# Delta-rule stage: joined scratch rows, a shared ring of gate weights, and another order of filler and block inversions

## The reference, cut to what matters

```
h = x + norm(W_o[ sig(gates_a) * (attention . W_a) + sig(gates_b) * (deltanet . W_b) ])
y = h + norm(relu(norm(h) W_1)^2 W_2)
```

```
lower = where(strict, beta * (k k^T) * decay, 0)
tinv  = (lower + I)^-1
u, w  = tinv @ (v * beta),  tinv @ (k * beta * exp(gc))
step:   v_new = u - w @ state
        o     = q_dec @ state + (q k^T * decay) @ v_new
        state = state * exp(g_last) + k_dec^T @ v_new
```

## Time and profile before

| what | value |
|---|---|
| median of 3 runs | 2793.87 us (2791.05 to 2799.13) |
| profiled execution, its own time | 2795.2 us |
| span from first to last instruction | 2793.4 us |
| mean granted clock of PE | 0.955 |
| PE busy over the span | 2533.9 us, 91% |
| DVE, ACT, POOL busy over the span | 1306.7, 863.4, 567.5 us |
| DMA, mean over the span | 134 GB/s |

### The profile page before, as it was taken

How to read it: one execution, slowest core, us unless ns; L and a number is a source line. 1 busy time by engine, 2 the same in 40 slices (tenths; PEclk the granted TensorE clock), 3 DMA queues, 4 the chain that set the end, 5 groups by cost and what they waited for, 6 DMA issues and landing times. The chain is left out here.

```text
span 2793.4 us, 33654 instructions
## 1 busy us (share of the span) xinstructions
PE 2533.9 (91%) x12600; PEld 2113.3 (76%) x12600; DVE 1306.7 (47%) x1688; ACT 863.4 (31%) x1415; POOL 567.5 (20%) x499
## 2 busy tenths in 40 slices
PE   6999999797989997998498894799999979999998
PEld 5888888686879895776287683688888768887887
DVE  5665125265635336887633433744444342234332
ACT  4333323251111115776300332322222142133221
POOL 2352236341212110000520231221121000000000
PEclk9999999898999999999599897999999989999999
DMA  4232212585555643221644554232232273345443
GB/s 142 72 91 87 77 53 106 166 260 185 163 158 170 177 135 144 102 102 68 226 141 147 198 176 168 73 98 79 89 97 79 76 254 103 115 145 206 162 150 106
DMA packets 308213, 373.38 MB, mean 134 GB/s; under 512 B 53240, under 2 KB 234616, under 8 KB 303480
## 3 DMA queue, kind: packets, MB, share of 16 engines
q1 hardware_dynamic: 216152, 293.97, 32.8%
q10 hardware_dynamic: 91936, 77.70, 8.5%
HBM read 251.98 MB, written 119.64 MB: 133 GB/s over the span
## 5 line engine op out<-in xcount | busy, mean ns | idle before, releaser
L2473 PE MATMUL y_ps<-w_hi,hid_hi 128*128 128x512 f32 x768 | 301.7, 393 | 23.9 <-DVE w_lo L2557 16.3
L2473 PE MATMUL y_ps<-w_lo,hid_hi 128*128 128x512 f32 x768 | 300.8, 392 | 0.0
L2473 PE MATMUL y_ps<-w_hi,hid_lo 128*128 128x512 f32 x768 | 300.6, 391 | 0.0
L2563 DVE TENSOR_TENSOR hid_lo<-ff_raw,hid_hi 128x1024 fp32r<-128x1024 f32 x96 | 114.0, 1223 | 320.6 <-ACT hid_hi L2527 320.4
L2527 ACT ACTIVATE hid_hi<-ff_raw 128x1024 fp32r<-128x1024 f32 x96 | 97.3, 1053 | 357.1 <-PE y_ps L2473 330.3
L2114 PE MATMUL ff_ps<-ffx_sums,w_ops 128*128 128x512 f32 x768 | 179.0, 392 | 15.7 <-DVE ffx_sums L2249 15.7
L2114 PE MATMUL ff_ps<-ffx_rest,w_ops 128*128 128x512 f32 x768 | 182.1, 393 | 8.3 <-DVE ffx_rest L2249 8.3
L2473 PEld LDWEIGHTS y_ps<-w_hi,hid_hi 128*128 128x128 f32 x768 | 145.5, 189 | 57.0 <-DVE w_lo L2557 17.8
L2114 PEld LDWEIGHTS ff_ps<-ffx_sums,w_ops 128*128 128x128 f32 x768 | 145.1, 189 | 47.1 <-issue 16.9
L2114 PEld LDWEIGHTS ff_ps<-ffx_rest,w_ops 128*128 128x128 f32 x768 | 145.7, 190 | 39.2 <-issue 8.7
L115 PE MATMUL proj_ps<-ht_hi,win_hi 128*128 128x512 f32 x576 | 172.9, 408 | 0.0
(11 more groups left out here) (255 smaller groups left out, 4899.6 us busy)
## 6 DMA issues: line engine op xcount, KB each, us to landing
ff_raw<-s_hid_s SPq DMA_DIRECT2D x96, 512.0 KB, 4.4
arena<-s_dn_s SPq DMA_DIRECT2D x24, 1024.0 KB, 5.7
s_hid_s<-ff_outs SPq DMA_DIRECT2D x96, 256.0 KB, 2.3
w_raw<-in_w_ff_in SPq DMA_DIRECT2D x16, 1024.0 KB, 5.7
ff_raw<-in_w_ff_out SPq DMA_DIRECT2D x32, 512.0 KB, 4.6
win_raw<-in_w_in SPq DMA_DIRECT2D x26, 512.0 KB, 3.4
s_made_s<-arena SPq DMA_DIRECT2D x12, 1024.0 KB, 5.5
arena<-s_made_s SPq DMA_DIRECT2D x48, 256.0 KB, 6.4
```

The source lines that it names most:

```text
L2473: mm = pe.matmul(acc[:, bank(u, t)], x[:, (t if opens(t) else kh), k], y[:, w], start=w == 0 and first == 0, stop=w == KF - 1 and first == 2)
L2563: dve.tensor_tensor(hlo[:, b, ks].rearrange("p k j -> p (k j)"), raw[:, r], f32(hhi[:, b, ks]).rearrange("p k j -> p (k j)"), ALU.subtract ...
```

## The change

- **Scratch layout.** `lb_s` and `inv_s` get an outer dimension for low or turned, so that tile, head and block number join into 64 rows: the transfers of `store_inverse` and `load_blocks` change from 4x16x1024 (or 64x1x1024) to 64x1024. In return `store_blocks` and `load_inverse` are split by that dimension: 8 transfers of 32x4x32 instead of 4 of 32x8x32.
- **Weight ring.** `raw`, `whi` and `wlo` are allocated in `program` and shared by `project` and `deltanet`. `project` has one raw buffer instead of two and loads and splits a 27th tile, the first of the 13, so that the first 72 filler matmuls of `deltanet` find their weights. The first token loads and POOL steps of `project` stand in another order.
- **Splits.** In `deltanet` the high part is made by ACT and the low part by DVE, at given segments; POOL has none.
- **Order.** wait 0, wait 1, make 0 to 7, then make 8 to 11 each followed by a wait, wait 6, and the steps. `FILL` is 20 in a make, 24 in a wait and 21 in a step: 408 before step -1 and 528 in the steps. PE's `sums` moves into wait 1.
- **Inversions.** Group 0 is done in three pieces, behind make 8, 9 and 10. Ten sub-steps of group 1 stand before the steps, the rest in iterations 0 to 5; group 2 takes iterations 6 to 12, with five sub-steps each, two before the mask and three after.
- **SP.** The stores of tiles 0 to 10 stand ahead of `store_inverse(0)`. Behind it come the blocks of group 1, inverse and low half of step 0, the identity, those of step 1, and the stores of tile 11. In the steps the second inverse is stored in iteration 6 instead of 5, the third in 13 instead of 14; the identity for group 2 is loaded in iteration 7 instead of 5.

```diff
-def deltanet(nc, io, ht_hi, ht_lo):
+def deltanet(nc, io, ht_hi, ht_lo, raw, whi, wlo):
...
-    ORDER = ([("make", t) for t in range(11)] + [("wait", n) for n in range(4)] + [("make", 11)] + [("wait", 4 + n) for n in range(4)] +
+    ORDER = ([("wait", n) for n in range(2)] + [("make", t) for t in range(8)] +
+             [x for n, t in enumerate(range(8, NT)) for x in (("make", t), ("wait", 2 + n))] + [("wait", 6)] +
...
-    FILL = {"make": 10, "wait": 24, "step": 25}
+    FILL = {"make": 20, "wait": 24, "step": 21}
...
-        PRE = 12
+        PRE = 10
...
-                        sp.dma_start(io["lb_s"][t, :, b].rearrange("x c t -> c x t"),
-                                     made[rows, t % 2, TURNED:LOW_F + 1, :, rows].rearrange("c x h t -> c (x h) t")).then_inc(blk_stored[t % 2], 16)
+                        for which in range(2):
+                            sp.dma_start(io["lb_s"][which, t, :, b].rearrange("h c t -> c h t"), made[rows, t % 2, TURNED + which, :, rows]).then_inc(blk_stored[t % 2], 16)
...
-                            sp.dma_start(io["inv_s"][d, t0:t0 + 4, which * NH:(which + 1) * NH].rearrange("t h b c j -> t (h b) (c j)"), src[rows]).then_inc(s["inv_stored"], 16)
+                            sp.dma_start(io["inv_s"][d, which, t0:t0 + 4].rearrange("t h b c j -> (t h b) (c j)"), src[rows]).then_inc(s["inv_stored"], 16)
...
-                        sp.dma_start(inv_in[rows, d, :, :, rows].rearrange("c w h j -> c (w h) j"), io["inv_s"][d, tile_of(d, u), :, b].rearrange("w c j -> c w j")).then_inc(inv_back[d], 16)
+                        for which in range(2):
+                            sp.dma_start(inv_in[rows, d, which, :, rows], io["inv_s"][d, which, tile_of(d, u), :, b].rearrange("h c j -> c h j")).then_inc(inv_back[d], 16)
...
-                    if v == 5:
+                    if v == 6:
                         store_inverse(1)
                         load_blocks(2)
+                    if v == 7:
                         sp.wait_ge(s["inv_stored"], 128)
                         load_identity()
-                    if v == 14:
+                    if v == 13:
                         store_inverse(2)
...
+                def keep_up(seg):
+
+                    for i in range(1, len(GATES)):
+                        if ready(i) + 1 == seg:
+                            dve.wait_ge(s["w_hi"], i)
+                            dve.tensor_tensor(wlo[:, i % 2], raw[:], f32(whi[:, i % 2]), ALU.subtract).then_inc(s["w_ready"], 1)
...
-                pool.wait_ge(w_in[n % 2], (n // 2 + 1) * 16)
+                pool.wait_ge(s["w_in"], (n + 1) * 16)
```

More of the change, by code:

```diff
@@ L142, with project @@
 EARLY_GATES = 3
-def project(nc, io, ht_hi, ht_lo):
+def project(nc, io, ht_hi, ht_lo, raw, whi, wlo):
     SLOT = {"k": 2, "q": 3}
@@ L154, in project @@
     N = len(TILES)
+    WEIGHTS = [col for _, _, col in TILES] + [GATE_COL + EARLY_GATES * P]
     GATING = 14
@@ L253, in _ @@
                 load_x(u, u)
-            for n in range(2):
-                load(n)
-            with sp.Fori(1, NT // 2) as i:
+            load(0)
+            for u in range(2):
+                load_x(u, 2 + u)
+            load(1)
+            with sp.Fori(2, NT // 2) as i:
                 for u in range(2):
                     load_x(u, i * 2 + u)
-            for n in range(2, N):
+            for n in range(2, N + 1):
                 load(n)
@@ L348, in _ @@
             root(0, 0)
-            for t, step, n in ((1, copy_hi, 0), (2, subtract_hi, 0), (3, copy_hi, 1), (4, subtract_hi, 1)):
+            for t, step, n in ((1, copy_hi, 0), (2, subtract_hi, 0), (3, None, 0), (4, None, 0), (5, copy_hi, 1), (6, subtract_hi, 1)):
                 root(t % 2, t)
-                step(n)
-            root(1, 5)
-            with pool.Fori(3, NT // 2) as i:
+                if step:
+                    step(n)
+            root(1, 7)
+            with pool.Fori(4, NT // 2) as i:
                 for u in range(2):
@@ L934, in finished, with ready @@
         return filled[seg + 1] // UNIT if seg >= 0 else 0
+    def ready(i):
+        return next((seg for seg in range(len(ORDER)) if finished(seg - 1) >= NG * (i - 1)), 0) if i >= 2 else 0
     def tile_of(d, s):
@@ L1120, in _ @@
                 sp.dma_start(level[:].rearrange("p a m j -> p (a m j)"), io["level_masks"]).then_inc(s["level_in"], 16)
-                for t in range(9):
+                for t in range(NT - 1):
                     if t + 3 < NT:
@@ L1129, in _ @@
                 load_blocks(1)
-                load_inverse(0)
-                load_inverse(1)
-                load_identity()
-                for t in range(9, NT):
-                    store_blocks(t)
-                    store_made(t)
                 for v in range(2):
+                    load_inverse(v)
                     load_low(v)
+                    if v == 0:
+                        load_identity()
+                store_blocks(NT - 1)
+                store_made(NT - 1)
                 for v in range(2):
@@ new lines, in keep_up @@
+                def keep_up(seg):
+                    for x in range(max(finished(seg - 2), 1), finished(seg - 1)):
+                        evict(x)
+                    for i in range(1, len(GATES)):
+                        if ready(i) == seg:
+                            act.wait_ge(s["w_in"], 16 * i)
+                            if i >= 2:
+                                act.wait_ge(s["f_done"], NG * (i - 1))
+                            act.activation(whi[:, i % 2], raw[:], ACT.Copy).then_inc(s["w_hi"], 1)
+                        if i > 1 and ready(i - 1) + 2 == seg:
+                            load_weights(i)
@@ L1511, in _ @@
                 dve.wait_ge(s["mask_done"], 3)
-                for t in range(9):
-                    make(t)
-                invert(0, 0, BLK - 1)
-                for t in range(9, NT):
-                    make(t)
+                for seg, (kind, n) in enumerate(ORDER):
+                    if kind == "step":
+                        break
+                    keep_up(seg)
+                    if kind == "make":
+                        make(n)
+                        if n in (8, 9, 10):
+                            invert(0, *((0, 11), (11, 21), (21, BLK - 1))[n - 8])
                 invert(1, 0, PRE)
@@ L1521, in _ @@
                         make_z(v)
+                    keep_up(SEG["step", v])
                     if after:
@@ L1589, in clear @@
                     pool.memset(side(inv_in[:, d, 0], d, BLK), 0.0).then_inc(s["cleared"], 1)
-                split()
                 pool.wait_ge(s["const_in"], 48)
@@ L1594, in _ @@
                     gate_hi(t)
-                split()
                 for seg, (kind, n) in enumerate(ORDER):
-                    keep_up(seg)
                     if kind == "make" and n + 2 < NT:
                         gate_hi(n + 2)
-                    if (kind, n) == ("wait", 4):
+                    if (kind, n) == ("step", -1):
                         pool.wait_ge(s["made_done"], NT)
```

107 lines of the change are left out of this document (45 added, 62 removed).

## The result

The changed kernel takes 2765.05 us (median of 4 runs, 2763.01 to 2766.47); the kernel before, beside it, 2793.98 (2791.05 to 2799.13). The ratio is 0.9894, with a 95% interval from 0.9879 to 0.991: about 29 us faster. 2764 was forecast. The profiled execution took 2763.01 us, its span is 2761.2; before it was 2795.2 and 2793.4, so the traces differ by 32.2.

What follows compares the result with a forecast made beforehand. PE's own work was taken to bound the stage, except at stalls of 50.8 us. Gains of 9 + 7.4 + 12.5 + 1 = 29.9 us took the profiled 2795.2 to 2765.3, or 2764 as median; range 2750 to 2782.

Steps and rivals of the forecast that it cites:

- The start: Start of the delta-rule stage: the first split gate weight carried over spares PE load and split, gaining 9 us (7.3 to 10.4).
- Before step -1: Preparations to step -1: two stalls go (22.8 us removed), new waits add 15.4, net gain 7.4 us (-3 to 13).
- D: End of the first inversions; step 0's inverse was forecast at D+15.7, the end of its mask's wait near D+26.
- The term of the two waits: Around step -1: PE newly waits 3.9 us for step 0's inverse and about 8.7 us for its mask.
- The 0.6 for a weight: Before step -1: 0.6 us of added PE waiting for a weight, counted among the new waits.
- The steps: Steps: stalls and half clock of 23.1 us go, a new wait and DVE's splits cost some, net gain 12.5 us (7 to 17).
- issued about 0.8 us behind those outputs: Iteration 6: group 2's identity is issued 0.8 us behind step 6's outputs, so PE stands for 6.3 us (4.5 to 7.6).
- Store to reload: Inverse's way through memory: with 64 joined rows, issue plus landing takes about 6.5 us (5 to 11) instead of 15.2.
- (a): Rival: the new waits are hidden, saving up to 12 us of 19.5, about 2752 us; chance 0.12.
- (b): Rival: joined rows do not spread over the DMA engines, the store still takes 15.2 us, about 2778 us; chance 0.08.
- (c): Rival: steps do not shrink, the period stays 14.25 us with 21 fillers, 2786 us; chance 0.12.
- (d): Rival: eight small loads a step hold up SP, binding from 1.47 us per issue; 2810 us at 2.0; chance 0.08.

Runs made afterwards that it cites:

- the early identity: Changed kernel with the identity for group 2 issued in iteration 6, ahead of step 8's inverse loads, instead of iteration 7: 2750.32 us, 2753.52 when run again.
- the other order before step -1: Changed kernel with SP issuing group 1's identity first behind the landed inverse store, and tile 11's stores ahead of step 1's inverse loads: 2760.18 us.

## Why the prediction was right, point by point

- **What bounds the kernel.** Right: the stalls that went were worth their time at the end, and 48 fillers moved out of the steps made no difference that the times show (2766.12 against 2765.05).
- **The start.** 9 forecast, 9.5 read. 7.0 of it is the earlier first matmul relative to the end of the projection; the rest is the clock and a gap of 0.45 us. PE is at half clock to 537.1 instead of 553.6.
- **Before step -1.** Both ends of the chain came within half a microsecond (D+15.5 and D+25.8 for D+15.7 and D+26.2). The second for its reason: the store of the last tile was the releaser. The first by luck: the inverse was there at D+13.0, 2.7 us earlier than forecast, and PE waited for the low half of the tile, whose landing the forecast left out. The term of the two waits was mis-sized: 9.0 us instead of 12.6. PE came at D+12.7 instead of 11.8, and eight fillers lie between the two stalls, not five; the first five ran at half clock, and with step 0's products they covered 4.6 instead of 2.1 us. The 0.6 for a weight did not appear. Net 12.4 instead of 7.4; 1.9 us of half clock behind the mask's wait, which the forecast has here, fall into the first step (15.24 instead of 13.31 us) and so into the next term.
- **The steps.** The period was right (13.31), and so were the 2 us for DVE's splits and sub-steps (0.27 + 0.73 + 0.71). The removed stalls came to 26.0 us instead of 23.1: before, five steps take 16.21, 15.66, 28.73, 14.73 and 20.99 us, where without a stall four of them are at 14.25 and the last at 13.36. The step that failed is "issued about 0.8 us behind those outputs". I looked at what stood ahead of the identity in SP's list but not at what held up the list: the load of step 8's inverse waits there for the landing of the second store. With 5.0 instead of 0.8 the iteration lost 12.4 us instead of 8.6; the net was 10.7 instead of 12.5: mainly 3.8 less here and 1.9 of clock from step -1, against 2.9 more of removed stalls.
- **Store to reload.** 6.5 forecast (5 to 11); 8.1 for the first group, and 11.7 for the second, which is out of the range, with the DMA engines busy all the time. The sign "landed within 7 us" was missed by both.
- **Rivals.** (a) did not come, as the waits that it would hide took 19.3 us (2.8, 6.2 and 10.3), but it was there to be had: the early identity and the other order before step -1 bring the kernel down to 2750 and 2760, both with group 2 later to 2742. (b) would have been dearer than 2778: without spreading the kernel takes 2785. (c) is out by the 13.31, and by the 12.86 with 19 fillers. (d) is out: the median issue of the eight loads was 0.44 us. The longest took 1.58, above the 1.4 that was named as a sign of being wrong, and the period did not grow.

The row of the eight loads, by the view of the tile, against the earlier trace rows:

```profile
L1090 SPq DMA_DIRECT2D inv_in<-s_inv_s x173: 318/444/1577, 689.7 to 983.8; - x173
```

One thing the forecast underrated: of the gain, 20 us of 29 by the medians, or 18.4 to 19.5 of 32.6 by the stage in the traces, hang on the layout. The list of waits named the transfers, and the DMA share of 0.26 the cause, but rival (b) prices the layout at 14 us (2778 for 2764).

## What to carry to other kernels

Where an engine waits for a transfer and the DMA share beside it is low (0.26 here for 4x16 rows), give the transfer an outermost dimension that spreads, by layout or by splitting it, before the order of work is touched. When a transfer is moved in a queue, go through every instruction ahead of it for what that one waits for, not only for how long its issue takes; and where an engine waits for several transfers, look which one lands last. And cross two parts of a change in all four combinations before crediting either.

## What the runs showed of the hardware that was not expected

- 16 stores of 16 rows (64 KB each) were issued at 0.46 us and took 11.2 us to the reload, four stores of 64 rows 8.1, four of 4x16 rows 15.2: number and size counted for less than how many engines moved (the DMA share over these stretches was 0.77, 0.88 and 0.31).
- The half clock at the start of the stage lasted 11.2 us before, behind an idle stretch of 13.26 us, but 3.5 us after one of 6.26 and 3.9 us after one of 10.35. Between the last two, which have the same fillers behind them, 4.1 us more of idle time made 0.4 us of difference; before, small matmuls and a gap of 0.45 us stood behind the first five fillers. What made the 11.2 us is not shown.
- Landing times of the same load depend on what else moves: the identity landed 6.8 us after its issue in the changed kernel, and 3.9 when issued ahead of the inverse's pieces.
